# A two-layer expert encoder: evictions by copy, the activation in place a stage later, and three smaller moves

## What is computed

```python
def peer(h, w_query, sub_keys, expert_down, expert_up):
    q = (x @ w_query).reshape(T, PEER_HEADS, 2, D_HALF)
    s = jnp.einsum('thcd,hckd->thck', q, sub_keys)
    s1, i1 = lax.top_k(s[:, :, 0], PEER_TOPK)
    s2, i2 = lax.top_k(s[:, :, 1], PEER_TOPK)
    ...                                   # 16 best of the sums: idx
    gate = jax.nn.softmax(top_s, axis=-1)
    a = jax.nn.gelu(jnp.einsum('cd,chkd->chk', xc, expert_down[ic]))
    return jnp.einsum('chk,chkd->cd', a * gc, expert_up[ic])
```

## Time and profile before

| | |
|---|---|
| three runs | 1921.91, 1924.6, 1925.65 us, median 1924.6 |
| the profiled execution | 1923.52 us |
| its span, first to last instruction | 1921.7 us |
| mean granted clock of TensorE | 0.996 of full speed |
| busy: PE, DVE, ACT, POOL | 98%, 73%, 52%, 36% of the span |

### The profile page before, as it was taken

One profiled execution on the slowest core, in us unless ns is written; L12 is line 12 of the kernel. 1 busy time (PEld: TensorE's weight loads), 2 busy tenths in 40 slices (PEclk: granted clock), 3 DMA queues, 4 the chain that ended last, 5 costly groups with the idle time before them and its releaser, 6 DMA issues.

```text
span 1921.7 us, 39006 instructions
## 1 busy us (share of the span) xinstructions
PE 1874.9 (98%) x12114; PEld 1703.6 (89%) x12114; DVE 1397.5 (73%) x3258; ACT 1007.6 (52%) x1638; POOL 696.9 (36%) x627
## 2 busy tenths in 40 slices
PE   7989999999999999999999999999999999999998
PEld 6879999999988888888889989999999988888887
DVE  5858788897467766667567778788897457667666
ACT  4644656656455455454444444666656454454453
POOL 1416687788730000000102106688788740000000
PEclk9999999999999999999999999999999999999999
DMA  6964565565568778996848844566565568778775
GB/s 233 340 249 154 177 185 177 174 179 185 185 217 250 240 240 276 292 304 213 279 159 303 308 155 153 177 185 179 172 186 179 183 206 257 240 239 242 240 241 190
DMA packets 159589, 419.99 MB, mean 219 GB/s; under 512 B 32427, under 2 KB 66251, under 8 KB 159020
## 3 DMA queue, kind: packets, MB, share of 16 engines
q1 hardware_dynamic: 130556, 369.23, 60.7%
q0 software_dynamic: 28976, 50.17, 7.7%
HBM read 382.30 MB, written 37.00 MB: 218 GB/s over the span
## 4 chain that ended last, share of the span: by engine, by line
PE 80%; ACT 6%; DVE 5%; issue 4%; POOL 4%; DMA 1%; SPq 0%; DVEq 0%; POOLq 0%; ACTq 0%
PE psum L1306 26%; PE psum L1308 25%; PE psum L1307 25%; POOL gates L405 4%; ACT L620 2%; ACT w_hi L471 2%; DVE w_lo L733 2%; ACT L662 1%; PE psum L1505 1%; PE psum L1476 1%; ACT big L620 1%; PE psum L1394 0%; DVE big L791 0%; PE psum L1405 0%; PE psum L1431 0%
## 5 line engine op out<-in xcount | busy, mean ns | idle before, releaser
L471 ACT CAST w_hi<-raw 128x1024 fp32r<-128x1024 f32 x636 | 662.9, 1048 | 341.7 <-PE psum L1308 328.8
L1306 PE MATMUL psum<-x_hi,w_hi 128*128 128x256 f32 x2576 | 738.6, 287 | 16.2 <-DVE w_lo L733 13.0
L1307 PE MATMUL psum<-x_lo,w_hi 128*128 128x256 f32 x2576 | 731.2, 284 | 0.0
L1308 PE MATMUL psum<-x_hi,w_lo 128*128 128x256 f32 x2576 | 731.2, 284 | 0.0
L405 POOL DMA_INDIRECT gates<-whole,address x512 | 622.4, 1216 | 246.7 <-issue 148.1
L1306 PEld LDWEIGHTS psum<-x_hi,w_hi 128*128 128x128 f32 x2576 | 496.6, 193 | 27.2 <-issue 12.9
L733 DVE TENSOR_TENSOR w_lo<-raw,w_hi 128x512 fp32r<-128x512 f32 x576 | 369.9, 683 | 178.9 <-ACT w_hi L471 178.5
L1307 PEld LDWEIGHTS psum<-x_lo,w_hi 128*128 128x128 f32 x2576 | 496.8, 193 | 0.9
L1308 PEld LDWEIGHTS psum<-x_hi,w_lo 128*128 128x128 f32 x2576 | 496.4, 193 | 0.0
L1306 PE MATMUL psum<-w_hi,l_hi 128*128 128x512 f32 x1152 | 452.2, 393 | 3.2 <-DVE l_lo L1233 2.2
L1308 PE MATMUL psum<-w_hi,l_lo 128*128 128x512 f32 x1152 | 448.8, 390 | 0.0
(11 more groups left out here) (144 smaller groups left out, 1122.8 us busy)
## 6 DMA issues: line engine op xcount, KB each, us to landing
raw<-in_down SPq DMA_DIRECT2D x256, 512.0 KB
raw<-in_up SPq DMA_DIRECT2D x256, 512.0 KB
raw<-in_sg_units SPq DMA_DIRECT2D x72, 512.0 KB
gates<-zeros POOLq DMA_DIRECT2D x64, 512.0 KB, 7.0
g_t<-gates SPq DMA_DIRECT2D x248, 128.0 KB, 4.5
raw<-in_query SPq DMA_DIRECT2D x32, 512.0 KB
raw<-in_attn_units SPq DMA_DIRECT2D x20, 512.0 KB
gates<-whole,address POOLq DMA_INDIRECT x512
```

Of the source, the lines that this page charges most:

```text
L471: act.copy(w_hi[n % SPLIT][:, :], raw[n % RAW][:, :]).then_inc(hi_done, 1)
L1306: pe.matmul(out_ap, hi_s, hi_m, start=start, stop=False)
L1307: pe.matmul(out_ap, hi_s, lo_m, start=False, stop=False)
L1308: return pe.matmul(out_ap, lo_s, hi_m, start=False, stop=stop)
```

## The change

Six edits, whose lines in the diff follow each other:

- `evict` copies the column to `acts` without gelu. The gelu runs later over `acts` in place (`activated`): the first eight columns at once in column 101, and from then on four columns at a time in each pass of the up stage's loop, one pass ahead. The semaphore `act_done` counts these, and DVE's `gate` waits for it.
- The gelu tables are no longer loaded in each slot, but once, in column 100. ACT loads 5 tables in the whole program, where there were 61.
- SP, not POOL, issues the store of `h` to `h_kept`, between the loads of query units 1 and 2, behind a wait for `h_done`.
- PE runs START_FILL = 30 transposes of `ident`, which nothing reads, before its first work.
- `x_landed` becomes one semaphore for each tile, so that ACT's squares of tile 0 wait for tile 0 alone. DVE still waits for both.
- DVE's two waits for `p1_read` ahead of the first gates give way to one for `act_done`.

```diff
+START_FILL = 30
@@ sync
             for t in range(TT):
-                sp.dma_start(h[:, t, :], x[t * P:(t + 1) * P, :]).then_inc(x_landed, 16)
+                sp.dma_start(h[:, t, :], x[t * P:(t + 1) * P, :]).then_inc(x_landed[t], 16)
...
-                stream(u["query"], QUERY_UNITS, rows(query_units[layer]))
+                queries = rows(query_units[layer])
+                for c in range(GROUP):
+                    if c == 2:
+                        sp.wait_ge(h_done, 4 * (2 * layer + 1))
+                        sp.dma_start(h_kept, h.rearrange("p t d -> p (t d)")).then_inc(h_stored, 16)
+                    load(u["query"] + c, queries(0, c))
+                stream(u["query"], QUERY_UNITS, queries, 1)
@@ gpsimd
-                pool.wait_ge(h_done, 4 * (2 * layer + 1))
-                pool.dma_start(h_kept, h.rearrange("p t d -> p (t d)")).then_inc(h_stored, 16)
                 scatter(layer)
@@ scalar
                     if c == 12:
                         exponentials(1)
-                        act.preload_act_table(ACT.Gelu_apprx_tanh)
...
                     act.wait_ge(used, i * group + (u["down"] + n + 1))
-                    act.activation(acts[:, bass.ds(i * group + n, 1), :], p1[n % P1_BANKS].rearrange("p (o t) -> p o t", o=1),
-                                   ACT.Gelu_apprx_tanh).then_inc(p1_read, 1)
+                    act.copy(acts[:, bass.ds(i * group + n, 1), :], p1[n % P1_BANKS].rearrange("p (o t) -> p o t", o=1)
+                             ).then_inc(p1_read, 1)
...
                         exponentials(item)
-                        act.preload_act_table(ACT.Gelu_apprx_tanh)
...
+                def activated(n, count, i=0):
+
+                    a = big[:, bass.ds(i * (GROUP * T) + n * T, count * T)]
+                    act.activation(a, a, ACT.Gelu_apprx_tanh).then_inc(act_done, 1)
...
                     evict(n)
+                    if n == searched:
+                        act.preload_act_table(ACT.Gelu_apprx_tanh)
+                    if n == searched + 1:
+                        act.wait_ge(p1_read, p["down"] + 2 * GROUP)
+                        activated(0, 2 * GROUP)
...
+                act.wait_ge(p1_read, p["down"] + NK)
                 with act.Fori(1, NK // GROUP - 1) as i:
                     for c in range(GROUP):
                         split_hi(u["up"] + c + AHEAD, i)
                         operand_hi(c + 1, i)
+                        if c == 0:
+                            activated(GROUP, GROUP, i)
@@ vector
+                    if n % GROUP == 0:
+                        dve.wait_ge(act_done, i + (layer * (NK // GROUP - 1) + n // GROUP))
...
-                dve.wait_ge(p1_read, p["down"] + GROUP)
+                dve.wait_ge(act_done, layer * (NK // GROUP - 1) + 1)
@@ tensor
             pe.wait_ge(made, 4)
+            for k in range(START_FILL):
+                pe.transpose(psum[:, 5, P * (k % 4):P * (k % 4) + P], ident[:, :], ident[:, :])
             pe.wait_ge(table_landed, 32)
```

More of the change, by code:

```diff
@@ L213, in build @@
         l_lo_done = sem("l_lo_done")
-        x_landed = sem("x_landed")
+        x_landed = [sem(f"x_landed{t}") for t in range(TT)]
         y_done = sem("y_done")
@@ L263, in build @@
         g_landed = [sem(f"g_landed{s}") for s in range(G_TILES)]
+        act_done = sem("act_done")
         gated_up = sem("gated_up")
@@ L297, in load, with stream @@
                 sp.dma_start(raw[n % RAW][:, :], source).then_inc(landed[n % RAW], 16)
-            def stream(first, count, source):
+            def stream(first, count, source, start=0):
                 passes = count // GROUP
-                start = 0
                 if first == 0:
@@ L475, in squares_first @@
                 if z == 0:
-                    act.wait_ge(x_landed, 16 * TT)
+                    act.wait_ge(x_landed[0], 16)
                 else:
@@ L482, in squares_second @@
             def squares_second(z):
-                if z:
+                if z == 0:
+                    act.wait_ge(x_landed[1], 16)
+                else:
                     act.wait_ge(h_done, 4 * (z - 1) + 3)
@@ L792, in residual @@
                 dve.wait_ge(h_done, 4 * n + 2 * t + 2)
-            dve.wait_ge(x_landed, 16 * TT)
+            for t in range(TT):
+                dve.wait_ge(x_landed[t], 16)
             dve.wait_ge(made, 7)
@@ L1255, in _ @@
                 first_operand_lo(3)
-                dve.wait_ge(p1_read, p["down"] + NK)
                 for n in range(GROUP):
```

## The result

The changed kernel takes 1905.25 us (median of 5 runs, 1903.88 to 1906.7), the kernel before 1924.71 (5 runs, 1921.91 to 1926.63): ratio 0.990, 95% interval 0.9885 to 0.9914. The gain is 19.5 us where 8.4 were forecast. The time lies in the range of the prediction, but at its fast end, where rival A stood: that it lies there is no credit to the mechanism that was forecast.

A forecast was written before the change was run, and what follows sets the result against it. PE, busy 98% of the span, was taken as the bound, so only its waits, refills and low clock count. Gains 0.3 + 7.5 + (4.05 - 1.3) + (0.45 - 2.6) = 8.4 us gave 1916.2 us, range 1905 to 1922.

The forecast's parts named there:

- rival A: Scatter: POOL follows, its series ends 6 us earlier in each layer; gain 20.4 us, time 1904; chance 0.13.
- The store moves to SP: 7.5 us gained: Layer 0, before the slots: DVE no longer waits for the store; PE's 4.9 us wait and some 2.6 for refill and clock go.
- rival B: Query stage: loads behind the store come late, PE waits up to 3 us in layer 0, 1 in layer 1; about 1920; chance 0.12.
- Tables out of the slots: 12.6 us offered: Search slots: without the two table loads each takes 20.16 us, not 20.61; 2 x 14 x 0.45 us offered.
- Little of it taken: Up stage: POOL's scatter gains only 0.45 us a layer; before clock losses, layer 0 gains 4.05 us, layer 1 0.45.
- Rival C: Slots: packed tighter, DVE holds POOL's writes more; slower by over 0.2% from 0.44 us a slot, 1933 at 0.6; chance 0.08.
- PE waits before half 1: Up stage: PE waits for POOL's last write, 2.3 us in layer 0, 5.9 in layer 1; 6.34 us from write to matmul.
- The clock after these waits: After the waits before half 1: a clock fall costs up to 2.6 us; 1.3 taken for layer 0, 2.6 for layer 1.
- The start: 0.3 us: Kernel start: 30 unread transposes may make PE fast for its first matmuls; 0.3 us gained, at most 0.66 before attention scores.

The follow-up runs named there:

- store_only_b: Kernel before with only the store of `h` issued by SP instead of POOL; 1918.07 us, ratio 0.9969 to the kernel before.
- act_delay_b: Kernel after with ACT copies of zeros, about 1.3 us, before and after each slot's exponentials, no table loads; 1912.08 us, one run (before 1926.52).
- phase_before: Kernel before with two POOL memsets behind the first write of layer 0's scatter series; 1925.18 us (before 1922.87).
- tables_back_d: Kernel after with the two table loads put back in every search slot; 1916.66 us, ratio 0.9968 to the kernel before.

## Why the prediction was wrong, step by step

*The store moves to SP: 7.5 us gained.* Right: 6.0 (4.0 to 7.9) by store_only_b, an interval that holds 7.5. In the stretch from which I took it, from the norm's first transposes on, it is 7.2: to the first exponential 24.7 us (111.62 to 136.3) for 31.9 (110.52 to 142.4). The stall of 4.9 us is gone, and no load behind the store was late (rival B): in store_only_b PE is busy for 11.93 of the 12 us from 118 to 130, at a granted clock of 1.00, where the kernel before had 7.09 and 0.89.

*Tables out of the slots: 12.6 us offered.* Right for the slot, which takes 20.16 us from exponential to exponential as forecast, for 20.61. It is 7.4 and 7.0 us from the first to the sixteenth and not 6.3: 13 slots of 0.45 lie between these, and the step from the second to the third exponential, at the border of the query stage, also became 1.6 and 1.2 us shorter (22.74 to 21.17, 22.60 to 21.37).

*Little of it taken.* This is the step that failed: "POOL gains only 0.45 of it: item 2, with which its series starts, lies behind one slot, and from there its own rate counts". I took POOL's rate as its own and so put the gain of the series at nothing. It was set by DVE, and DVE's pile by ACT's loads. Without the loads the series takes 331.7 us and PE's waits of 2.3 and 5.9 us before half 1 do not come. Against rival A I had put "nothing in the change takes work off POOL during the series"; true of work, but what left was held time, 21 us in layer 0 and 26 in layer 1, of which 12.9 and 16.8 shortened the series; the rest, 8.5 and 9.4, POOL now spends waiting, nearly all of it for its pace. The evidence stood in the prediction: 0.96 or 1.31 us for the same write, and two lengths for the same series. Rival C used the exclusion with the wrong sign. It counted how much DVE is idle in a slot, which the change hardly alters, and not how the idle time lies: 2.97 us in one piece and then a pile, or a little before each split.

*PE waits before half 1.* The mechanism is real. In act_delay_b, where the slots are nearly as short as in the kernel after and the series is long, the wait is there in layer 0, 2.00 us where I had 2.3:

```profile
545.83 1.57 POOL L414 DMA_INDIRECT gates<-whole,address  x1 [0.30 <-issue]
```

```profile
552.36 0.50 PE L1338 MATMUL psum<-w_hi,l_hi 128*128 128x512 f32 x1 [2.00 <-DVE l_lo L1277]
```

From write to matmul it is 6.53 us, for my 6.34 (6.81 by my way of adding what this longer write took). Layer 1, where I had 5.9, shows none in this run; its series was 344.0 and not 348.5. In the kernel after the last write comes 12.9 us sooner in its series than in the kernel before, and nothing waits for it.

*The clock after these waits.* Without the waits there was nothing to fall. For layer 0 half the price was too much: behind the wait of 2.00 us in act_delay_b the granted clock stays at 1.00 (552.3 to 560.0). No run shows a wait near 5.9 us at this place, so the 2.6 of layer 1 is untested. What was lost instead, 2.2 us between the layers and 1.3 behind the last slot, is about what single executions differ by: phase_before, which changes neither stretch, shows 1.8 more than the kernel before between the layers (457.3 to 1155.1), and behind the last slot the quiet runs lie from 0.4 under it to 1.4 over it.

*The start: 0.3 us.* Nothing of it is to be seen. The first products come at 13.26 for 13.46 and run at the lower pace in both kernels (0.41 us a matmul), and the first attention scores, the place where I had put the gain, begin at 32.90 for 32.70. Single executions place the first exponential within 2 us of each other for nearly the same start (133.9 and 135.9 us in after and tables_back_d), so a gain of 0.3 could not be told by the time.

## What to carry to other kernels

An engine's rate read from a trace is its own only if its instructions have one length. Where the same instruction comes with two, ask which engine it shares something with, and by what rhythm that one works. Work taken off one engine can speed up a third that it never touches: not because the second does less, but because it no longer idles and then catches up. When all changes at once make a surprise, put the suspected part back alone, and then put mere work in its place.

## What the runs showed of the hardware

- How long POOL's writes are held depends on how DVE's two-input operations are packed, not on how many there are: the same DVE work, busy for 260 us of the series in either kernel, with and without a pile gave 57 and 36 us held in 224 writes.
- After 30 unread transposes the 16 of the first norm took 1.97 us, and without them 3.68. Unread transposes also kept the granted clock at 1.00 (22 of them over 2.56 us, from 10.29 on, behind 46 others with the two matmuls of the bias row between them), and 3.16 us without work let it fall to 0.50; 2.00 us without work, in act_delay_b, did not. The Trainium skill says that transposes do not count for the clock gate (TensorE: Matmul & The Clock Gate, Part 4: PE-mode transpose); these traces say otherwise.
- Chips differ: on five of eight every kernel took 4 to 5% longer. In these traces PE has short waits that nothing in the profile explains, 29 to 54 us in all, and a mean granted clock of 0.976 to 0.984; on the quiet ones these waits come to at most 0.2 us, and the clock is 0.995 to 0.998. The slots' part, worth 0.73% on a quiet chip, showed as 0.25 and 0.42% there, the store's 0.31% as 0.09%.
